# A two-block transformer kernel on one core: splits, roots and evacuations in another order at three places of block one, and memory keys divided 1:3 around the last feed-forward rows

## What is computed

```python
    # block one
    h = modulate(rmsnorm(x, norm1_g[i]), shift1, scale1)
    z = h @ w_in[i] + b_in[i]
    u, v, val, gate = jnp.split(z, [D_A, 2 * D_A, 2 * D_A + D_B], axis=-1)
...
    y = jnp.concatenate([rmsnorm(y_a, out_norm_a_g[i]), rmsnorm(y_b, out_norm_b_g[i])], axis=-1)
    x = x + gate1[:, None, :] * (y @ w_out[i])
    h2 = modulate(rmsnorm(x, norm2_g[i]), shift2, scale2)
    g_ff, up_ff = jnp.split(h2 @ w_ffn_in[i], 2, axis=-1)
    x = x + gate2[:, None, :] * ((jax.nn.silu(g_ff) * up_ff) @ w_ffn_out[i])
    return modulate(rmsnorm(x, norm_f_g), shift_f, scale_f)
    # block two
    h = rmsnorm_2(x, mix_norm[l])
    z = h @ w_in[l]                      # queries, keys, values, index queries (qi), 72 more columns (kw)
    x = x + jnp.concatenate([y_pool, y_attn], axis=-1) @ w_out[l]
    # memory cross-attention: k, v from rmsnorm(mem) @ w_kv
    # experts: silu(h @ w_gate) * (h @ w_up) @ w_down, 32 of them
```

## Times and profile before

| | us |
|---|---|
| median of 3 runs | 857.55 (856.64 to 860.73) |
| the profiled execution | 856.41 |
| its span, first to last instruction | 854.2 |
| TensorE busy / DVE busy / ScalarE busy | 727.6 / 392.1 / 325.4 |
| mean granted TensorE clock | 0.919 of full |

### The profile page before, as it was taken

How to read it: one execution, slowest core, us unless ns; L and a number is a source line. 1 busy time by engine, 2 the same in 40 slices (tenths; PEclk the granted TensorE clock), 3 DMA queues, 4 the chain that set the end, 5 groups by cost and what they waited for, 6 DMA issues and landing times.

```text
span 854.2 us, 12600 instructions
## 1 busy us (share of the span) xinstructions
PE 727.6 (85%) x5259; PEld 581.6 (68%) x5260; DVE 392.1 (46%) x741; ACT 325.4 (38%) x587; POOL 22.4 (3%) x53
## 2 busy tenths in 40 slices
PE   6599999689999999999879987886769867868766
PEld 5376777588999999999768775765664623625422
DVE  1537996437544555455537798354351110111002
ACT  2336563526444444445445655464521111101001
POOL 4000010000000020000000000000000000000000
PEclk8799999889999999999858998898969989989988
DMA  9998974329777445643223350470378999999994
GB/s 336 397 409 328 408 290 105 98 69 326 246 243 247 154 148 198 222 152 135 99 99 96 114 191 7 154 296 0 126 318 358 420 420 421 420 422 421 420 421 167
DMA packets 68465, 211.41 MB, mean 248 GB/s; under 512 B 7159, under 2 KB 31381, under 8 KB 52022
## 3 DMA queue, kind: packets, MB, share of 16 engines
q1 hardware_dynamic: 67362, 209.91, 64.3%
q0 software_dynamic: 800, 0.63, 0.5%
q10 hardware_dynamic: 244, 0.03, 0.0%
HBM read 209.51 MB, written 1.05 MB: 247 GB/s over the span
## 4 chain that ended last, share of the span: by engine, by line
PE 60%; DMA 19%; DVE 8%; ACT 5%; SPq 4%; issue 2%; ACTq 0%; DVEq 0%
PE ps L1833 10%; PE ps L1834 10%; PE ps L1835 10%; DMA ring<-in_expert_w_up_dram 10%; PE ps L1843 5%; PE ps L1844 5%; PE ps L1845 5%; SPq L395 4%; DMA ring<-in_expert_w_down_dram 3%; DMA Z<-in_expert_w_up_dram 3%; PE ps L2441 3%; DMA ring<-in_w_in_dram 2%; PE ps L1895 2%; DVE LO L1089 2%; PE ps L1990 2%
## 5 line engine op out<-in xcount | busy, mean ns | idle before, releaser
L1089 DVE TENSOR_TENSOR LO<-ring,HI 128x1024 fp32r<-128x1024 f32 (+1 forms) x135 | 163.7, 1221 | 127.6 <-ACT HI L604 127.4
L604 ACT ACTIVATE HI<-ring 128x1024 fp32r<-128x1024 f32 (+1 forms) x135 | 141.0, 1054 | 144.1 <-PE ps L1835 70.4
L2441 PE MATMUL ps<-ring,ZM 128*32 128x256 f32 x832 | 79.1, 439 | 25.5 <-DMA ring<-in_expert_w_gate_dram 13.0
L1833 PE MATMUL ps<-AH,HI 128*128 128x256 f32 x320 | 91.0, 285 | 0.1
L1834 PE MATMUL ps<-AL,HI 128*128 128x256 f32 x320 | 90.5, 283 | 0.0
L1835 PE MATMUL ps<-AH,LO 128*128 128x256 f32 x320 | 90.5, 283 | 0.0
L1833 PE MATMUL ps<-HI,AH 128*128 128x512 f32 (+1 forms) x176 | 72.1, 409 | 16.5 <-DVE AL L1107 6.2
L2441 PEld LDWEIGHTS ps<-ring,ZM 128*32 128x32 f32 x832 | 37.2, 125 | 57.8 <-DMA ring<-in_expert_w_gate_dram 18.5
L1834 PE MATMUL ps<-LO,AH 128*128 128x512 f32 (+1 forms) x176 | 70.6, 401 | 0.0
L1835 PE MATMUL ps<-HI,AL 128*128 128x512 f32 (+1 forms) x176 | 70.5, 400 | 0.0
L1843 PE MATMUL ps<-AH,HI 128*128 128x256 f32 x192 | 58.4, 304 | 11.8 <-DVE LO L1089 6.4
(11 more groups left out here) (368 smaller groups left out, 1292.8 us busy)
## 6 DMA issues: line engine op xcount, KB each, us to landing
ring<-in_expert_w_down_dram SPq DMA_DIRECT2D x32, 1024.0 KB, 26.7
ring<-in_expert_w_gate_dram SPq DMA_DIRECT2D x26, 1024.0 KB, 26.7
ring<-in_expert_w_up_dram SPq DMA_DIRECT2D x26, 1024.0 KB, 27.0
ring<-in_ada_w_dram SPq DMA_DIRECT2D x24, 1024.0 KB, 14.0
ring<-in_w_ffn_in_dram SPq DMA_DIRECT2D x20, 1024.0 KB, 7.1
ring<-in_w_in_dram SPq DMA_DIRECT2D x18, 1024.0 KB, 8.8
ring<-in_w_ffn_out_dram SPq DMA_DIRECT2D x11, 1024.0 KB, 7.4
ring<-in_w_out_dram SPq DMA_DIRECT2D x8, 1024.0 KB, 7.1
```

The source lines that it names most:

```text
L604: act(HI[:, i % UNITS, 0:w], W.view(name)[:, o:o + w], ACT.Copy).then_inc(s_hi, 1)
L1089: tt(LO[:, i % UNITS, 0:w], W.view(name)[:, o:o + w], HI[:, i % UNITS, 0:w].bitcast(F32), ALU.subtract).then_inc(s_lo, 1)
L1833: mm(dst, lh, rh, start=start, stop=False)
L2441: ins = mm(ps[b][CAP * j:CAP * j + CAP, 256 * h:256 * h + 256], XG[:, k, P * q + CAP * j:P * q + CAP * j + CAP], W.view(name)[:, 256 * k:2 ...
```

## The change

- split_order and the loads: in_v0, in_v1 (2 units each) become in_v0, in_v1, in_v2 with 1, 2 and 1 units; in_v0 is loaded ahead of the last of the first eight condition loads. kv_k0, kv_k1 become kv_k0, kv_k1, kv_k2, likewise 1, 2, 1.
- value projection: unit 0 is split right behind the root, ahead of the condition's columns; the next splits stand between the k of AH and AL; TensorE waits for AL by k.
- output projection: three splits move ahead of Silu (two low parts ahead of the group multiply), the fourth behind the root; the column transposes of condition 3 move behind the sums; k = 4 runs alone ahead of k = 5 to 7.
- keys: the last feed-forward rows follow key unit 0, the sums unit 1, the spread unit 2; unit 3 follows the spread.
- queries: the sums for SUM_MIX, their root and reciprocal move behind kw; kw's split moves ahead of the key squares; the wait for the root moves from all transposes to the last (XTB order 4, 1, 3, 5); TensorE waits for AL by k.

```diff
@@ split_order
-    out = [f"{w}{h}" for w in ("in_v", "in_g", "in_u", "in_w", "kv_v") for h in "01"]
+    out = ["in_v0", "in_v1", "in_v2"] + [f"{w}{h}" for w in ("in_g", "in_u", "in_w", "kv_v") for h in "01"]
...
-    out += ["kv_k0", f"fo{NPAIR - 1}", "kv_k1", "qi0", "qi1", "kw"]
+    out += ["kv_k0", f"fo{NPAIR - 1}", "kv_k1", "kv_k2", "qi0", "qi1", "kw"]
...
-XTB = (4, 5, 1, 3)
+XTB = (4, 1, 3, 5)
@@ SP
-            ada(A["ada_w"], 0, range(8), 0)
-            rows128("in_v0", w_in, 1024, 512, 0, 4)
-            rows128("in_v1", w_in, 1024, 512, 4, 4)
+            ada(A["ada_w"], 0, range(7), 0)
+            rows128("in_v0", w_in, 1024, 512, 0, 2)
+            ada(A["ada_w"], 0, (7,), 0)
+            rows128("in_v1", w_in, 1024, 512, 2, 4)
+            rows128("in_v2", w_in, 1024, 512, 6, 2)
@@ ScalarE
             rooted(RTS[0], ps[4][:, 0:2], SUM_X)
-            hi_to(1)
+            hi_to(0)
...
-                if k == 3:
-                    hi_to(2)
+                if k in (1, 4):
+                    hi_to(1 + k // 4)
...
                 act(VM[:, t, :], ps[(2, 6)[t]][:, :], ACT.Copy).then_inc(s_vm, 1)
+            for i in (1, 2, 3):
+                hi_to(io + i + AHEAD)
...
             warm(ACT.Sqrt)
-            for i in (1, 2):
-                hi_to(io + i + AHEAD)
             rooted(RTS[2], ps[2][:, 0:2], SUM_B)
+            hi_to(io + 4 + AHEAD)
...
-            for i in (3, 4):
-                hi_to(io + i + AHEAD)
...
+            hi_to(ik + 2 + AHEAD)
+            rooted(RTS[4], ps[2][:, 0:2], SUM_F)
             hi_to(ik + 3 + AHEAD)
-            rooted(RTS[4], ps[2][:, 0:2], SUM_F)
...
-            rooted(rs[:, :], ps[5][:, 0:2], SUM_MIX)
+            hi_to(ik + 7 + AHEAD)
...
             for i in range(4):
                 hi_to(S.first["qi0"] + i + 3)
+            rooted(rs[:, :], ps[5][:, 0:2], SUM_MIX)
             ac.wait_ge(s_rs, 1)
@@ DVE
+            lo_to(0)
             condition(1, 7)
...
-            lo_to(1)
...
-                if k == 4:
-                    lo_to(2)
+                if k in (2, 5):
+                    lo_to(1 + k // 4)
...
             recip(RGS, SUM_G)
+            for i in (1, 2):
+                lo_to(io + i + AHEAD)
...
-            for i in (1, 2):
-                lo_to(io + i + AHEAD)
+            lo_to(io + 3 + AHEAD)
+            recip(RTS[2], SUM_B)
             columns(3, 6, C2[:, B1 + 16:B1 + 32])
...
-            recip(RTS[2], SUM_B)
             rows_scaled(YB, 4, OB, ps[2][:, 256:512], RB_B)
-            for i in (3, 4):
-                lo_to(io + i + AHEAD)
+            lo_to(io + 4 + AHEAD)
...
-            ve.wait_ge(s_rn, SUM_MIX)
-            ve.reciprocal(rs[:, :], rs[:, :]).then_inc(s_rs, 1)
+            lo_to(ik + 7 + AHEAD)
...
-            lo_to(S.first["kw"] + 3)
             ve.wait_ge(s_kn, 2)
             ve.reciprocal(mst[:, 8:16], mst[:, 8:16]).then_inc(s_kn, 1)
+            ve.wait_ge(s_rn, SUM_MIX)
+            ve.reciprocal(rs[:, :], rs[:, :]).then_inc(s_rs, 1)
+            lo_to(S.first["kw"] + 3)
@@ TensorE
-                    if low is None:
-                        te.wait_ge(s_al, op + per * (i + 1))
-                    else:
+                    if low is None and per == 1:
+                        te.wait_ge(s_al, op + i + 1)
+                    if low is not None:
                         te.wait_ge(low, i + 1)
...
+                            if low is None and per == 2 and t == 0:
+                                te.wait_ge(s_al, op + k + 1)
...
-                    te.wait_ge(s_al, OP_X + 2 * q + 2)
...
+                            if ct == 0:
+                                te.wait_ge(s_al, OP_X + k + 1)
...
                 if k == 2:
-                    te.wait_ge(s_vm, 2)
-                    columns(3, 6)
                     te.wait_ge(s_rr, SUM_G)
...
                 te.wait_ge(s_sqs, SQ_B + k // 2 + 1)
+                if k == 0:
+                    te.wait_ge(s_vm, 2)
                 added_up(2, SQY[:, k, :], k, 4)
+            columns(3, 6)
             spread(2, 256, 2, SUM_B)
 
+            te.wait_ge(s_lo, io + 5)
+            te.wait_ge(s_al, OP_Y + 5)
+            for m in range(8):
+                ins = projected(4, m, False, False)
+            ins.then_inc(s_un, 1)
             te.wait_ge(s_lo, io + 8)
             te.wait_ge(s_al, OP_Y + 8)
             for m in range(8):
-                for k in range(4, 8):
+                for k in range(5, 8):
...
             def between_keys(i):
-                if i == 1:
+                if i == 0:
...
-                if i == 2:
+                if i == 1:
...
+                if i == 2:
+                    te.wait_ge(s_xu, 16)
+                    spread(4, 0, 4, SUM_F)
...
-            strip(("qi0", "qi1"), (0, 2), OP_MIX, 0, None, between_qi, per=2)
+            strip(("kv_k0", "kv_k1", "kv_k2"), (1, 3), 0, 0, None, between_keys, MH, ML, low=s_ml)
+            strip(("qi0", "qi1"), (0, 2), OP_MIX, 0, per=2)
...
+            for k in range(8):
+                te.wait_ge(s_sqs, SQ_M + k + 1)
+                added_up(5, SQ2[:, k, :], k, 8)
             te.wait_ge(s_ks, 10)
-            te.wait_ge(s_rs, 1)
             for i in range(4):
+                if i == 3:
+                    te.wait_ge(s_rn, SUM_MIX)
```

More of the change, by code:

```diff
@@ L90, in split_order @@
         out += [f"fg{i + 1}", f"fo{i}", f"fu{i + 1}"]
-    out += ["kv_k0", f"fo{NPAIR - 1}", "kv_k1", "qi0", "qi1", "kw"]
+    out += ["kv_k0", f"fo{NPAIR - 1}", "kv_k1", "kv_k2", "qi0", "qi1", "kw"]
     out += [f"{w}{h}" for w in ("q", "k", "v", "u", "pool", "attn", "wq", "wo") for h in "01"]
-    return [(n, 8 * (NZ - 2560) if n == "kw" else 2048) for n in out]
+    width = {"kw": 8 * (NZ - 2560), "in_v0": 1024, "in_v2": 1024, "kv_k0": 1024, "kv_k2": 1024}
+    return [(n, width.get(n, 2048)) for n in out]
 T0 = {n: i + 1 for i, n in enumerate(("u1", "kvv", "kvk", "qi", "kw", "q", "k", "v", "u", "pool0", "pool1",
@@ L462, in _ @@
                 if i == NPAIR - 1:
-                    rows128("kv_k0", w_kv, 0, 512, 0, 4)
+                    rows128("kv_k0", w_kv, 0, 512, 0, 2)
                 load(f"fo{i}", split_until(f"fo{i}"), (lambda s: kn(s, 2, D),
                      w_fo[256 * i:256 * i + 256, :].rearrange("(j p) n -> p j n", p=P)))
-            rows128("kv_k1", w_kv, 0, 512, 4, 4)
+            rows128("kv_k1", w_kv, 0, 512, 2, 4)
+            rows128("kv_k2", w_kv, 0, 512, 6, 2)
             for h in range(2):
@@ L822, in _ @@
             ik = S.first["kv_k0"]
-            for i in range(3):
+            for i in range(2):
                 hi_to(ik + i + AHEAD)
@@ L845, in _ @@
                 else:
-                    ac.wait_ge(s_un, S.end["kv_k1"])
+                    ac.wait_ge(s_un, S.end["kv_k2"])
                 for h in range(4):
@@ L1346, in _ @@
             ik = S.first["kv_k0"]
-            for i in range(3):
+            for i in range(2):
                 lo_to(ik + i + AHEAD)
             added_tiles(3, "fo10", (4, 5, 6, 7), colv[:, 2, 8:16])
+            lo_to(ik + 2 + AHEAD)
+            recip(RTS[4], SUM_F)
             lo_to(ik + 3 + AHEAD)
-            recip(RTS[4], SUM_F)
             lo_to(ik + 4 + AHEAD)
@@ L1961, in _ @@
             te.wait_ge(s_xc, 4)
-            by_channel(("in_v0", "in_v1"), lambda ct: ps[ct][:, 0:256], "value", (0, 1, 2, 3), lambda q: q and ada(1, q - 1))
+            by_channel(("in_v0", "in_v1", "in_v2"), lambda ct: ps[ct][:, 0:256], "value", (0, 1, 2, 3), lambda q: q and ada(1, q - 1))
             te.wait_ge(s_r2, 16 * LOADS2)
@@ L2191, in between_keys @@
                         added_up(2, SQX[:, m, :], m, 8)
+                if i == 2:
+                    te.wait_ge(s_xu, 16)
+                    spread(4, 0, 4, SUM_F)
             te.wait_ge(s_at, NF - 2)
-            strip(("kv_k0", "kv_k1"), (1, 3), 0, 0, None, between_keys, MH, ML, low=s_ml)
-            te.wait_ge(s_xu, 16)
-            spread(4, 0, 4, SUM_F)
-            def between_qi(i):
-                if i == 3:
-                    for k in range(8):
-                        te.wait_ge(s_sqs, SQ_M + k + 1)
-                        added_up(5, SQ2[:, k, :], k, 8)
-            strip(("qi0", "qi1"), (0, 2), OP_MIX, 0, None, between_qi, per=2)
+            strip(("kv_k0", "kv_k1", "kv_k2"), (1, 3), 0, 0, None, between_keys, MH, ML, low=s_ml)
+            strip(("qi0", "qi1"), (0, 2), OP_MIX, 0, per=2)
             u, w72 = S.first["kw"], NZ - 2560
```

## The result

The changed kernel takes 845.08 us (median of 4 executions, 843.22 to 846.79) against 858.51 for the kernel before beside it (856.64 to 860.73): a ratio of 0.9842, interval 0.9805 to 0.9879. A second series gave 841.94 against 859.24, 0.9795 (0.9762 to 0.9827). So the gain is 13.4 to 17.3 us where 18.6 were forecast. The profiled execution took 843.22 with a span of 841.1 us, against 856.41 and 854.2: 13.1 us less span.

The account below looks back on a forecast made before the run. TensorE gaps before 614 us were taken as the bound, with the expert-weight tail moving along. Gains of 2.35 + 6.5 + 9.75 = 18.6 us took the profiled 856.41 to 837.8, a median of 839.0; range 833 to 846.

Parts of the forecast that it names:

- Carry to the end: Expert-weight tail: whatever the first 614 us give back moves the whole tail forward, one for one.
- First place: Value projection: first matmul at 35.25 instead of 37.6, gain 2.35 us, with ends of 0 and 3.6.
- scale at 33.9: Value projection: the half load costs the last condition block 1.3 us, so its scale is written at 33.9 us.
- I let all of it through: Value projection: the whole 2.35 us gain lives on, as loads have caught up and slots come free earlier.
- Second place: Output projection, second half: first k=4 matmul at 166.4 instead of 172.9, gain 6.5 us, from 4.9 to 7.5.
- 4.4 to 4.7 behind: Output projection: the root follows Silu's start at 158.45 by 4.4 to 4.7 us, at 163.1.
- Places three and four: Keys, queries, 72-column products, root and transposes: first q matmul at 441.0, together 9.75 us gain; place three alone 4.7.
- (a): Rival at kw and the sums: both keep the high clock, another 4.4 us, 834.6 us; chance 0.14.
- (b): Rival at the value projection: no gain, since half loads hold the queue or the condition block is later; 841.3 us; chance 0.10.
- (c): Rival in places three and four: a new order of waits eats half, 4.9 us less, 843.9 us; chance 0.14.
- (d): Rival, slower: the clock stays low behind the sums for query, q and k strips, costing 28.8 us, 867.8 us; chance 0.02.
- (e): Rival: gaps only move, as waits for low parts stay last at each place; 855 us, within 4 us; chance 0.05.

Follow-up runs that it names:

- multiply first: Changed kernel, with DVE doing the group multiply ahead of the two low parts of the output weights: 843.27 us, ratio 0.9784.
- The dummy products: Changed kernel plus four dummy 512-column products on TensorE ahead of the last adaptation block, nothing left out: 842.78 us, ratio 0.9814.
- the kernel with place two alone: Kernel before with only the output projection's changes (splits, low parts, k = 4 alone): 852.8 us, ratio 0.9925.
- the keys-first run: Changed kernel, DVE's key products ahead of its wait for the root, residual copies ahead of the third q unit's low part: 838.62 us, ratio 0.9775.
- the kernel with all three: Changed kernel with half load behind the condition block, group multiply ahead of low parts, and key products ahead of the root wait: 835.76 us, ratio 0.9733.
- the last kernel: Changed kernel with all three variations, but the sums for SUM_MIX back ahead of kw: 835.94 us, ratio 0.9719.

## Why the prediction was right, and where it was off

**The whole.** The forecast was 18.6 us of gain; the profiled executions give 13.1 in the span. The measured time lies in the range, at its upper side, in the first series. Of the missing 5.5 us, 3.4 are the first place with what followed it up to k=0, 0.5 the second, and 1.7 are three stretches that were to keep their length. The ledger divides the 13.1: up to k=0 -1.07, k=0 to k=4 6.03, from there to the memory keys -0.63, then to the q strip 9.85, to the expert issue -0.41, behind it -0.67.

**Carry to the end: right.** The tail was forecast to move one for one; 14.2 us at the q strip gave 13.8 at the expert issue and 13.1 in the span. Over all profiled executions the q strip starts anywhere from 428.7 to 453.9, and from there to the end it takes 400.6 to 404.5 us in all but one (409.1, multiply first).

**First place: right at the load, wrong at the scale, and worth nothing at the end.** The half load was to cost the block 1.3 us and cost 1.45. The Trainium skill, "DMA: Bandwidth & Descriptors", section "Anatomy of one DMA — SWDGE (gpsimd) path", gives a fixed cost of about 2.0 us for a DMA that GpSimd issues; added here, that is an estimate of 3.3 us for the block. These loads are issued by SyncE, into a full queue, and their trace, with 1.45, shows no such addition. The step that failed is "scale at 33.9": it took block and transposes at their old durations. The idle time ahead of them grew from 1.25 to 2.77 us, the clock fell, and block and transposes took 0.86 and 0.46 more; 1.45 + 0.86 + 0.46 is the 2.8 us by which the scale is late. The dummy products show this cause: without the idle time both are back at 1.07 and 0.66. The second failure is "I let all of it through": it treats the low clock of 3.0 us behind the start as a fixed delay. The first fast matmul came at 40.58 against 40.66, and 0.56 us of gain were left at the strip of keys and values. Up to k=0 another 1.63 went. Timeline of TensorE, before and after:

```profile
132.89 1.92 PE L1909 MATMUL ps<-avg,Z 128*128 128x1 f32 x16 [1.98 <-ACT Z L749]
```

```profile
132.34 3.31 PE L1918 MATMUL ps<-avg,Z 128*128 128x1 f32 x16 [1.98 <-ACT Z L753]
```

The same 16 sums behind the same wait of 1.98 take 1.92 us once and 3.31 the other time. The stretch from the strip to k=0 took 16.4, 18.0 or 19.6 us in all profiled executions, the kernel before showing the first two, the kernels with the changed first place all three, seven times of nine the last; the three kernels with some other part of the change and without the first place show 18.0 twice and 19.6 once. Whether that is chance or follows from the first place isn't settled.

**Second place: right, 6.03 for 6.5.** The wait for four low parts is gone as forecast, and AL is last, 2.63 behind the spread (2.66 forecast). The cost of the move is right too: counted from VM, Silu starts 1.47 later than in the earlier trace rows, for 1.55 forecast, since the first low part can't begin before the first of three splits is done (156.44), and the multiply stands behind both. The term that was off is the root, "4.4 to 4.7 behind" Silu: it came 5.16 behind. Before, the sums between them followed other work of TensorE at a granted clock of 1.00. Timeline of TensorE before:

```profile
159.90 1.84 PE L1909 MATMUL ps<-avg,Z 128*128 128x1 f32 x16
```

After, they start behind 1.49 us of idle time, the granted clock is 0.66 from 163 to 164 us and 0.50 behind that, and they take 2.47 us. In the kernel with place two alone the same sums behind the same idle time took 1.95, the root came 4.63 behind Silu, and the stretch gave 6.59. So here too the sum left out what the clock may take. The run with the multiply first removed Silu's delay and the idle time ahead of the sums.

**Places three and four: right, 9.85 for 9.75**, with errors that cancel. Place three (memory keys to end of queries) gave 4.28 for 4.7. For kw 7.4 us were forecast and 6.3 came: its clock fell 4.2 us in, where the forecast took about 3 (granted clock 1.00 to 418 us, 0.83 from 418 to 420, 0.50 behind). In the second series it fell only behind kw, 5.3 us in all. The sums took 6.8 for 6.1. The chain root to key transposes took 6.69 for 6.7. That chain was priced as a cost that can't be avoided, and the keys-first run shows that 2.26 of it can.

**The rivals.** (a) came true in part: kw kept the high clock for most of its time, the sums did not. (b) is what happened at the first place, by another mechanism than either of its two: neither the queue nor the block's transfer, but the clock. (c) and (d) show nowhere: the query strip has no wait over 0.4 us, and the q strip has the fast matmul again at 439.98, 3.4 us in. (e) didn't come either: the waits for low parts were not the last ones any more.

## What to carry to other kernels

Price a stall on TensorE together with the clock it leaves behind: a gap that grew from 1.25 to 2.77 us made the twelve matmuls behind it take 1.7 to 1.8 times as long, and an earlier start was worth only as much as the clock's return came earlier. When a split is moved ahead of a chain, move it ahead only of what can't start yet: two of the three variations tried here are plain cases of work (key products, the group multiply) that could have gone earlier and stood behind work that waited for something else. What their stretches gave, about 2 us each, shows in the profiles; in the medians only the kernel with all three lies clear of the change. Where single executions differ by 3 us at one anchor, judge a change of 1 to 2 us by the stretch between two anchors of the profile, and the whole by medians.

## What the runs showed of the hardware

One-column matmuls were followed by the low clock although they are issued back to back: over the 32 sums at 392.13 the granted clock was 0.93, and over the 4 us behind 396 it was 0.64. 72-column ones kept the high clock for 4.2 us in one execution of the changed kernel and for all of their 5.3 us in the other; behind the sums, in the last kernel, they kept it for 1.8.

From the first value matmul to the clock's return it took from 2.9 us (35.43 to 38.32, all three variations) to 6.4 us (36.73 to 43.12, multiply first) in stretches of nearly the same code, leaving aside the run with the dummy products, where the granted clock was 1.00 from 24 to 48 us. From the same matmul to the strip of keys and values it is 87.5 us in the first of these two executions and 90.6 in the second: this is how a late return moves what follows.
